# Shared key part rotated once, rotated parts transposed in pairs, and two norms taken in halves

## The reference, cut to what matters

```python
def rms_norm(x, gain):
    xf = x.astype(jnp.float32)
    y = xf * lax.rsqrt(jnp.mean(xf * xf, axis=-1, keepdims=True) + NORM_EPS)
    return (y * gain.astype(jnp.float32)).astype(x.dtype)

# in mla_attention, 8 heads; a part without position (128) and a rotated part (64) per head
a = h @ w_a
cq, ckv, k_pe = jnp.split(a, [MLA_Q_LORA, MLA_Q_LORA + MLA_KV_LORA], axis=-1)
q = (rms_norm(cq, q_a_gain) @ w_qb).reshape(b, s, MLA_HEADS, MLA_QK_DIM)
kv = (rms_norm(ckv, kv_a_gain) @ w_kvb).reshape(b, s, MLA_HEADS, MLA_NOPE + MLA_V)
k_nope, v = kv[..., :MLA_NOPE], kv[..., MLA_NOPE:]
k_pe = jnp.broadcast_to(k_pe[:, :, None, :], (b, s, MLA_HEADS, MLA_ROPE))
k = jnp.concatenate([k_nope, k_pe], axis=-1)
q = rms_norm(q, q_gain)
k = rms_norm(k, k_gain)
q = jnp.concatenate([q[..., :MLA_NOPE], rope(q[..., MLA_NOPE:], pos)], axis=-1)
k = jnp.concatenate([k[..., :MLA_NOPE], rope(k[..., MLA_NOPE:], pos)], axis=-1)

# second_block: mod = silu(c) @ w_ada + b_ada gives shifts, scales and gates of two modulated norms
h = modulate(rms_norm_2(x, g_attn), sh1, sc1)
...
return rms_norm_2(x, g_final)
```

## Time and profile before

| | |
|---|---|
| median of 3 runs | 1501.66 us (1500.86 to 1502.32) |
| profiled execution | 1501.71 us |
| its span | 1500.0 us |
| TensorE busy in the span | 1301.6 us (87%) |
| VectorE, ScalarE, GpSimd busy | 666.0, 273.8, 131.6 us |
| latent heads and attention | about 598 to 696 us |
| norm ahead of the hybrid mixer | about 1161 to 1167 us |
| last norm and store | about 1492 to 1500 us |

### The profile page before, as it was taken

How to read it: one execution, slowest core, us unless ns; L and a number is a source line. 1 busy time by engine, 2 the same in 40 slices (tenths; PEclk the granted TensorE clock), 3 DMA queues, 4 the chain that set the end, 5 groups by cost and what they waited for, 6 DMA issues and landing times.

```text
span 1500.0 us, 25645 instructions
## 1 busy us (share of the span) xinstructions
PE 1301.6 (87%) x9730; PEld 806.1 (54%) x9730; DVE 666.0 (44%) x1622; ACT 273.8 (18%) x756; POOL 131.6 (9%) x201
## 2 busy tenths in 40 slices
PE   9999999766776679999999766776679999999997
PEld 4455565433443344665665433443344875899943
DVE  3874634221222123682633221122123646699976
ACT  2153211100010001362211100010000235222200
POOL 1312000000000000210100000000000133222100
PEclk9999999988898899999999898898889999999999
DMA  8979799999999999959899999999999992654400
GB/s 292 401 283 341 289 422 404 421 421 422 422 421 422 422 422 398 365 204 420 321 420 401 421 420 422 422 422 422 423 422 401 384 365 66 211 169 169 169 29 28
DMA packets 120555, 513.63 MB, mean 342 GB/s; under 512 B 12296, under 2 KB 46796, under 8 KB 69144
## 3 DMA queue, kind: packets, MB, share of 16 engines
q1 hardware_dynamic: 118576, 507.30, 84.7%
q0 software_dynamic: 1728, 5.12, 1.0%
q10 hardware_dynamic: 168, 0.09, 0.0%
HBM read 511.39 MB, written 1.08 MB: 342 GB/s over the span
## 4 chain that ended last, share of the span: by engine, by line
PE 58%; DMA 19%; SPq 17%; issue 3%; DVE 2%; ACT 1%; ACTq 0%; POOL 0%; POOLq 0%; DVEq 0%
DMA ring<-in_moe_w_up 15%; SPq L1872 13%; PE bank L1415 9%; PE bank L575 9%; PE bank L2689 8%; PE bank L2724 4%; PE bank L1430 4%; DMA BC<-in_moe_w_up 3%; PE bank L1401 3%; PE bank L1443 3%; PE bank L453 3%; PE bank L2314 3%; PE bank L465 3%; SPq L1881 3%; PE bank L723 2%
## 5 line engine op out<-in xcount | busy, mean ns | idle before, releaser
L1415 PE MATMUL bank<-ring,hT 128*32 128x256 f32 (+1 forms) x2848 | 280.6, 451 | 131.9 <-DMA ring<-in_moe_w_up 65.6
L1415 PEld LDWEIGHTS bank<-ring,hT 128*32 128x32 f32 (+1 forms) x2848 | 147.9, 131 | 233.2 <-issue 170.0
L1707 DVE TENSOR_SCALAR pT<-pT 128x256 f32<-128x256 f32 x34 | 10.0, 294 | 408.1 <-ACT pT L1839 408.1
L1415 PE MATMUL bank<-BC,hT 128*32 128x256 f32 (+1 forms) x1120 | 148.4, 436 | 43.6 <-DMA ring<-in_moe_w_up 22.1
L1401 PEld LDWEIGHTS bank<-gtab,hn 128*128 128x128 f32 x1088 | 129.3, 192 | 15.4 <-issue 14.3
L1401 PE MATMUL bank<-gtab,hn 128*128 128x128 f32 x1088 | 132.5, 275 | 0.1
L1415 PEld LDWEIGHTS bank<-BC,hT 128*32 128x32 f32 (+1 forms) x1120 | 74.8, 127 | 83.5 <-issue 66.5
L1430 PE MATMUL bank<-ring,gtab 128*32 128x512 f32 (+1 forms) x768 | 116.8, 596 | 1.8 <-DMA ring<-in_moe_w_down 1.3
L1443 PE MATMUL bank<-hT,A 128*128 128x512 f32 x256 | 118.3, 605 | 0.0
L575 PE MATMUL bank<-ring,hT 128*128 128x512 f32 (+3 forms) x288 | 99.6, 505 | 0.3 <-DVE hT L314 0.2
L1839 ACT ACTIVATE pT<-bank 128x256 f32<-128x256 f32 x34 | 13.1, 384 | 461.3 <-PE bank L1415 461.3
(11 more groups left out here) (390 smaller groups left out, 1948.3 us busy)
## 6 DMA issues: line engine op xcount, KB each, us to landing
ring<-in_moe_w_gate SPq DMA_DIRECT2D x90, 1024.0 KB, 25.1
ring<-in_moe_w_up SPq DMA_DIRECT2D x88, 1024.0 KB, 25.5
ring<-in_moe_w_down SPq DMA_DIRECT2D x88, 1024.0 KB, 26.3
BC<-in_moe_w_gate SPq DMA_DIRECT2D x38, 1024.0 KB, 24.7
BC<-in_moe_w_up SPq DMA_DIRECT2D x32, 1024.0 KB, 25.0
BC<-in_moe_w_down SPq DMA_DIRECT2D x28, 1024.0 KB, 26.2
ring<-in_w_ada SPq DMA_DIRECT2D x24, 1024.0 KB, 14.1
ring<-in_w_up SPq DMA_DIRECT2D x22, 1024.0 KB, 7.3
```

The source lines that it names most:

```text
L1415: i = nc.tensor.matmul(GATE[q * cap:(q + 1) * cap, part * FF:(part + 1) * FF], xg[:, c, q * cap:(q + 1) * cap], u[:, c, :], start=(c == 0) ...
```

## The change

There are four parts.

1. The key's rotated part is rotated once, ahead of the pairs (four instructions on 128 elements of each partition), and no longer for each of the four key pairs. The scaling writes the rotated parts of two heads side by side into `turned_ropes`, so that one transpose of 128 columns turns both. Even heads' fills carry the pair, and odd heads' fills have two transposes only. Two copies, of partitions 0 to 63 and 64 to 127, take the pair out. Zeros now lie on the other half of the partitions for odd heads.
2. All key fills are copied out by VectorE, partly between its own steps, and all query fills by ScalarE. The order of fills changes, TensorE's `cond2` matmuls stand in one piece behind the eighth fill, and VectorE's last `cond2` sum stands behind the scaling in its step `j == 3`. GpSimd, not ScalarE, issues the store of the `cond2` row.
3. `n3` takes its squares in four halves. A second half is read from the PSUM bank itself, and VectorE's copy of that bank waits until ScalarE has read it.
4. The last norm squares tile 0 in two halves, of which the first is squared as soon as it is complete. VectorE multiplies by the gain while the root is being made and by the root afterwards in two halves, each with a store of its own.

```diff
@@ norm_stage, close_vector_ahead
+            def square_halves(act, tt):
+                for nb in range(2):
+                    nc.scalar.activation(hn[:, tt, nb * NB:(nb + 1) * NB], half_rows(act, tt, nb), ACT.Square, scale=D ** -0.5,
+                                         accum_out=half_sums[:, 2 * tt + nb:2 * tt + nb + 1]).then_inc(squares.sem, 1)
...
-            for nb in range(2):
-                for tt in range(TT):
-                    products.add(dve, tt, nb)
+            for tt in range(TT):
+                products.add(dve, tt, 0)
+            for tt in range(TT):
+                norm.squared(dve, 2 * (tt + 1))
+                products.add(dve, tt, 1)
             for tt in range(TT):
                 norm.scale(dve, tt)
                 norm.evac(dve, tt, 0)
...
+            def half_rows(eng, tt, nb):
+
+                if nb == 0:
+                    eng.wait_ge(*added(tt + 1))
+                    return X[:, tt, 0:NB]
+                eng.wait_ge(*summed(tt + 2))
+                return bank[2 * tt + nb][:, :]
@@ heads_vector
+            cs, sn = (gtab[:, 1, k, :, :] for k in range(2))
+            nc.vector.tensor_tensor(k_rope, k_rope_in, cs, ALU.mult)
+            nc.vector.tensor_tensor(k_rope_2[:, :, 0:32], k_rope_in[:, :, 32:64], sn[:, :, 0:32], ALU.mult)
+            dv.done(nc.vector.tensor_tensor(k_rope_2[:, :, 32:64], k_rope_in[:, :, 0:32], sn[:, :, 32:64], ALU.mult))
+            dv.done(nc.vector.tensor_tensor(k_rope, k_rope, k_rope_2, ALU.add))
...
+                turned = k_rope.unsqueeze(2).broadcast_to([P, TT, n, ROT]) if qk else t1s[j % 2]
...
-                nc.vector.tensor_tensor(x[:, :, :, NOPE:], t1s[j % 2], r.broadcast_to([P, TT, n, ROT]),
+                nc.vector.tensor_tensor(turned_ropes[j].rearrange("p t (h d) -> p t h d", h=n), turned, r.broadcast_to([P, TT, n, ROT]),
                                         ALU.mult).then_inc(l_qk.sem, 1)
...
+                if not qk:
+                    rotate_queries(j)
+                if j == len(l_items) - 1:
+                    keys_turned(dve, 0, 2)
                 if j >= 1:
                     scale_heads(j - 1)
+                if j == 3:
+                    cond2.vector(dve, 1)
+            keys_turned(dve, 2, 4)
             scale_heads(len(l_items) - 1)
@@ t4
-            l_jobs.append((lambda tt, x=x, h=h: x[:, tt, h, 0:NOPE], P, nopeT[:, h, k, :], mla_gain[:, 5 + k:6 + k]))
-            l_jobs.append((lambda tt, x=x, h=h: x[:, tt, h, NOPE:], ROT, peT[0:ROT, h, k, :], None))
+            fill = [(lambda tt, x=x, h=h: x[:, tt, h, 0:NOPE], P, nopeT[:, h, k, :], mla_gain[:, 5 + k:6 + k])]
+            if h % 2 == 0:
+                fill.append((lambda tt, k=k, h=h: turned_ropes[4 * k + h // 2][:, tt, :], P,
+                             [((0, ROT), peT[0:ROT, h, k, :]), ((ROT, P), peT[ROT:P, h + 1, k, :])], None))
+            l_jobs.append(fill)
...
-        t4 = turn_stage("t4", lambda pe: None, l_jobs, by=[f for f, (k, h) in enumerate(l_order) if k == 0 or h < 2],
+        t4 = turn_stage("t4", lambda pe: None, l_jobs, by=[f for f, (k, h) in enumerate(l_order) if k == 0],
                         fill_ready=l_normed, banks=(4, 5, 6, 7))
...
             pe.wait_ge(*pkv.copied(8))
-            cond2.tensor(pe, 4, 6)
-            t4.tensor(pe, 4, 6)
-            cond2.tensor(pe, 6, 8)
-            t4.tensor(pe, 6)
+            t4.tensor(pe, 4, 8)
+            cond2.tensor(pe, 4, 8)
+            t4.tensor(pe, 8)
@@ last norm
+            act.wait_ge(*out_added(3))
+            square_out(act, 0, NB, D, 1)
+            act.wait_ge(*out_added(4))
+            square_out(act, 0, 0, NB, 2)
...
+            dve.wait_ge(*out_added(4))
+            nc.vector.tensor_tensor(hn[:, 0, :], X[:, 0, :], g_fin, ALU.mult).then_inc(gained.sem, 1)
+            dve.wait_ge(*gained(1))
+            dve.wait_ge(*last_rs(2))
+            for n in range(2):
+                o = hn[:, 0, n * NB:(n + 1) * NB]
+                nc.vector.tensor_scalar(o, o, last_root[:, 0:1], None, ALU.mult).then_inc(result.sem, 1)
...
-            for k, tt in enumerate(last_order):
+            for k, (tt, a, b) in enumerate(((1, 0, D), (0, 0, NB), (0, NB, D))):
                 sp.wait_ge(*result(k + 1))
-                sp.dma_start(out[0, tt * P:(tt + 1) * P, :], hn[:, tt, :]).then_inc(final_out.sem, 16)
+                sp.dma_start(out[0, tt * P:(tt + 1) * P, a:b], hn[:, tt, a:b]).then_inc(final_out.sem, 16)
@@ ScalarE and GpSimd
-            t4.scalar(act, 0, 6)
-            cond2.scalar(act)
-            t4.scalar(act, 6)
+            t4.scalar(act, 0, 8)
+            cond2.copy(act)
+            t4.scalar(act, 8)
...
             heads_gpsimd(pool)
+            cond2.store(pool)
             m2.gpsimd(pool)
```

More of the change, by code:

```diff
@@ L259, in build, with norm_stage @@
             tensor = vector = scalar = gpsimd = sync = staticmethod(lambda eng: None)
-        def norm_stage(tile_ready, gain, shift=None, extra=(), late_root=False):
+        def norm_stage(tile_ready, gain, shift=None, extra=(), late_root=False, half_rows=None):
             st = Stage()
-            squares, rooted = shared("norm_squares", TT), shared("norm_rooted", TT)
+            parts = 2 if half_rows else 1
+            squares, rooted = shared("norm_squares", parts * TT), shared("norm_rooted", TT)
+            half_sums = stat[:, 4:4 + 2 * TT]
             scaled = shared("norm_scaled", 0 if late_root else TT)
@@ L377, in close_scalar_ahead @@
             for tt in range(TT):
-                norm.square(act, tt)
+                norm.square_halves(act, tt)
             for tt in range(TT):
@@ L656, in evac @@
                         ps = bank[banks[f % len(banks)]][0:w, k * S:(k + 1) * S]
+                        if isinstance(dst, list):
+                            for (a, b), part in dst:
+                                copy = nc.vector.tensor_copy
+                                i = nc.scalar.activation(part, ps[a:b, :], ACT.Copy) if scalar else copy(part, ps[a:b, :])
+                            continue
                         if scalar and scale is not None:
@@ L1148, in ready @@
                 eng.wait_ge(*self.stored(16))
-        cond1, cond2, cond3 = Conditioning(0, 3), Conditioning(1, 3, 5), Conditioning(2, 3)
+        cond1 = Conditioning(0, 3)
+        cond2 = Conditioning(1, 3, 5, cond1)
+        cond3 = Conditioning(2, 3, DC, cond2)
         cond1.plan(DC)
@@ L1996, in copy_a @@
             return nc.scalar.activation(hn[:, tt, n * NB:n * NB + ps.shape[1]], ps, ACT.Copy, scale=n2.rstd[:, tt:tt + 1])
-        pe_zeroed = shared("cleared", 1)
+        pe_zeroed = shared("cleared", 2)
         a_sq, a_rs = shared("sum_sq", 4), shared("sum_rs", 2)
@@ L2145, in l_normed, with keys_turned @@
             pe.wait_ge(*l_qk(4 * k + h // L_HEADS + 1))
-        t4 = turn_stage("t4", lambda pe: None, l_jobs, by=[f for f, (k, h) in enumerate(l_order) if k == 0 or h < 2],
+        t4 = turn_stage("t4", lambda pe: None, l_jobs, by=[f for f, (k, h) in enumerate(l_order) if k == 0],
                         fill_ready=l_normed, banks=(4, 5, 6, 7))
+        def keys_turned(dve, first, last):
+            for h in range(first, last):
+                t4.vector(dve, l_order.index((1, h)), l_order.index((1, h)) + 1)
         K5, Q7, K6, K7 = (l_order.index(kh) for kh in ((1, 5), (0, 7), (1, 6), (1, 7)))
@@ L2176, in rotary_zero_gpsimd @@
             pool.wait_ge(*n2.rooted(TT))
-            nc.gpsimd.memset(BC[ROT:P, 16 * S:32 * S], 0.0).then_inc(pe_zeroed.sem, 1)
+            zero = BC[:, 16 * S:32 * S].rearrange("p (h o s) -> p h o s", h=HEADS // 2, o=2)
+            for odd in range(2):
+                nc.gpsimd.memset(zero[ROT * (1 - odd):P - ROT * odd, :, odd, :], 0.0).then_inc(pe_zeroed.sem, 1)
         def latents_ready(pe):
-            pe.wait_ge(*pe_zeroed(1))
+            pe.wait_ge(*pe_zeroed(2))
         def latent_head(h):
@@ L2907, in last_scale @@
[L2907 to L2912 removed]
+        last_sq, last_rs, result = shared("sum_sq", 3), shared("sum_rs", 2), sem("result")
+        out_sums, last_root = stat[:, 4:7], stat[:, 2:2 + TT]
@@ new lines, in build, with square_out @@
+        squared_out = hT[:, :, :].rearrange("p (t c) s -> p t (c s)", t=TT)
+        gained = shared("picked", 1)
+        def square_out(act, tt, a, b, k):
+            nc.scalar.activation(squared_out[:, tt, a:b], X[:, tt, a:b], ACT.Square, scale=D ** -0.5,
+                                 accum_out=out_sums[:, k:k + 1]).then_inc(last_sq.sem, 1)
+        def last_scalar(act):
+            act.wait_ge(*out_added(2))
+            square_out(act, 1, 0, D, 0)
+            act.wait_ge(*out_added(3))
+            square_out(act, 0, NB, D, 1)
+            act.wait_ge(*out_added(4))
+            square_out(act, 0, 0, NB, 2)
@@ new lines, in last_gpsimd @@
+        def last_gpsimd(pool):
+            r = last_root[:, 1:2]
+            pool.wait_ge(*last_sq(1))
```

(6 more changed lines are left out.)

98 lines of the change are left out of this document (53 added, 45 removed).

## The result

The changed kernel takes 1507.81 us, the median of 7 runs (1506.4 to 1509.25); the kernel before, run beside it, 1502.21 (7 runs, 1500.86 to 1503.47). The ratio is 1.0038, 95% interval 1.0028 to 1.0048: slower by more than the 0.2% that can be told apart, and outside my range of 1499.0 to 1503.7. The profiled execution took 1509.25 us with a span of 1507.5; before it was 1500.0.

A forecast was written before the change was run, and what follows sets the result against it. TensorE (58% of the chain) and waits for weights were taken to bound the kernel. From 1501.71 us, +1.4 (latent heads), -0.15 (norm ahead of the hybrid mixer) and -1.35 (last norm) gave 1501.6 us, range 1499.0 to 1503.7.

The forecast's parts named there:

- Second mixture: Mixture behind the latent heads: the heads' +1.4 us reaches the end 1:1, the mixture's length changing only by the shift.
- a change of the mixture's length: Sign against the forecast: the mixture behind the latent heads changes its length by more than the shift.
- Heads, the order: Latent heads: 1.9 us of transposes saved, 3.3 us of waits uncovered that `cond2` had covered; +1.4 us.
- rival 3: Latent heads: TensorE's clock falls after the idle times, adding 3.5 to 5 us, so 1505 to 1506.6 us; chance 0.08.
- To the router: Scores to second router: no added time; the third score's last query copies come before its turn.
- n3: Norm ahead of the hybrid mixer: half squares bring the scaling slightly sooner; -0.15 us, bounds -0.4 and +0.4.
- the wait named: Norm ahead of the hybrid mixer: tile 1's second copy waits for all four squares; scaling tile 0 first gives about 1.1 us.
- Last norm: Kernel's end: last store issued 0.75 us sooner and its transfer 0.6 shorter; -1.35 us, ends -1.7 and -0.6.
- The case in which GpSimd stands until VectorE's product ends: Last norm: GpSimd is held by VectorE's multiplication by the gain; the term would be -1.1 us.
- Range: Whole kernel: terms' bounds with run spread gave 1499.8 to 1503.5 us; stated range 1499.0 to 1503.7.

The follow-up runs named there:

- e5: Changed kernel with 6 warming matmuls in the first mixture replaced by 15 narrower, moving the second mixture's loop to instruction 7367; 1504.99 us, ratio 1.0023 to before.
- e6: Kernel before without 8 warming matmuls in the first mixture, moving the second mixture's loop from instruction 7364 to 7332; 1507.55 us, ratio 1.0033 to before.
- e10: Kernel before without 2 of 6 warming matmuls in the first mixture's last block, second mixture's loop from instruction 7356; 1505.08 us, one execution.
- e11: Kernel before without 4 of 6 warming matmuls in the first mixture's last block, second mixture's loop from instruction 7348; 1507.26 us, one execution.
- e3: Changed kernel with two warming matmuls (results unused) in TensorE's first wait in the latent heads; 1506.78 us, ratio 1.0030 to before.
- e8: Kernel before with only the norms changed, tile 0 scaled before tile 1's squares, only the last norm's first half multiplied by gain ahead; 1500.28 us, ratio 0.9989.
- e7: Changed kernel with the edits of e4 and e5 together: conditioning sum moved into the wait, loop shifted by narrow warming matmuls; 1502.37 us, ratio 1.0005 to before.
- e4: Changed kernel with the `cond2` matmuls moved into TensorE's first wait and ScalarE's row copy behind its second query fill; 1504.57 us, ratio 1.0015 to before.

## Why the prediction was wrong, step by step

- **Second mixture: the step that failed.** I wrote that the delay reaches the end and "I count it 1:1", so the mixture would keep its length. It grew by 3.66 us, alone more than my range allowed. Shown by e5, e6, e10 and e11: the shorter stream moved TensorE's loop over an edge behind which its blocks are fetched again in each pass. That it then touches eight blocks and not seven is worked out from its length and the edge. I counted the transposes that leave as time and not as instructions ahead of a loop; the row of the instruction queue was on the page, with just as many packets as the stream has blocks. I had named a change of the mixture's length as what would prove me wrong, without a cause for it. It was not the only step: with mixture 2 as forecast the measured terms still add up to +2.4, or 1504.1 from 1501.66, 0.4 above my range, and only with the clock as forecast too do they give +0.9 and 1502.5. The same rows leave one thing open: TensorE's waits of 11.3 us turn into 3.7 us of a stretch that waits for weights. Between 900 and 1100 us 83.83 MB of weights came instead of 84.38; at 421 GB/s that is 1.3 us, and I did not find the rest in bytes.
- **Heads, the order:** +1.4 forecast, +1.50 at full clock (e3). The playing through of banks and copies was right in place and size.
- **Heads, the clock (rival 3, given 0.08):** it came, at 1.54 us instead of 3.5 to 5. The reason that I gave against it was the 3.07 us that left the clock alone; here 2.34 and 0.45 us, with four records of work between, did not. It cost less than I said since the clock was back at 658.6, before half of the conditioning sum was done.
- **To the router:** 0 forecast, +0.50. The fourth score waits 0.38 us for the split key copy, now one of 128 and two of 64 partitions, and the next product 0.25 behind it; I had followed the query copies only. All kernels with the new heads have it, 61.88 to 61.90 against 61.37 to 61.40.
- **n3:** −0.15 forecast, −0.39 measured, inside its bounds, and the wait named was the right one: e8 took it away for another 0.67, where I had put this at about 1.1.
- **Last norm:** −1.35 forecast, −0.74 measured. The half square is right (0.63). GpSimd lost 0.39 instead of 0.2, so the last store was issued 3.07 us after the last addition instead of 3.49, 0.42 sooner where I had 0.75. It landed 0.3 to 0.4 us sooner, not 0.63: 256 KB at 401 GB/s are 0.65 of its 2.2 us. The case in which GpSimd stands until VectorE's product ends, for which I had -1.1, came in kind (it ended 0.18 behind the product) and nearer in size than the 0.2 that I took from the row. e8 shows the same beside an instruction with one large input.
- **Sum:** with mixture 2, clock and way to the router put in, 1.50 + 1.54 + 0.50 + 3.66 − 0.39 − 0.74 = +6.1 us, against 5.6 between the medians.
- **Range:** the upper bounds of my terms, +2.4, +0.4 and -0.6, add up to 1503.9 and not to the 1503.5 that I gave them. Nothing turns on it, since 1507.81 lies above both.

## What to carry to other kernels

Before removing or adding instructions on an engine that runs a large loop, count how long the loop is in its stream and by how much its start moves: 33 instructions fewer cost 3.0 to 3.7 us of the mixture here, and the remedy was some 32 idle ones. (Between the medians the remedy was worth 2.8 us, e5 against the changed kernel, and 2.2, e7 against e4.) Where the blocks begin the stream does not say; shifting the loop and counting packets does. If a page's instruction queue shows more packets than the stream has blocks, a loop is being fetched again, and the waits on "issue" at its turns are the sign. When work is moved out of a gap, play through which wait it had covered, and then ask what the clock does on both sides of that wait.

## What the runs showed of the hardware

- TensorE kept a loop of 1655 instructions when it touched 7 blocks of 16 KB, and fetched its blocks again in each pass when it touched 8, nine packets a pass; two turns cost 3.0 to 3.7 us in a stretch bound by weights, with 3.3 to 4.6 us of wait for each block that was late and 8.8 and 9.0 where two were late in a row.
- The granted clock fell to 0.50 after 2.34 us idle, 0.6 us of work and 0.45 us idle, and was 1.00 again from about 658.6, after steady work; it cost 1.54 us (e3).
- A GpSimd instruction on 128x1 elements that starts beside a VectorE instruction of 1.22 or 0.75 us which reads SBUF ends 0.17 to 0.18 us after that one: 0.57 and 0.79 us instead of 0.31.
